# Moving the first tile's routing ahead of the second tile's last work in a two-block transformer kernel

## The reference, cut to what matters

```python
def peer_ffn(h, w_pq, sub_keys, u_tab, v_tab):          # for each token, 8 heads
    q = (xc @ w_pq).reshape(P_CHUNK, P_HEADS, 2, P_DK // 2)
    s = jnp.einsum('thpd,hpkd->thpk', q, sub_keys)
    s_top, i_top = lax.top_k(s, P_TOPK)                  # 16 of 128, for each half
    cand = s_top[..., 0, :, None] + s_top[..., 1, None, :]
    best, ci = lax.top_k(cand.reshape(P_CHUNK, P_HEADS, P_TOPK * P_TOPK), P_TOPK)
    ...
    expert = e1 * N_KEYS + e2
    gate = jax.nn.softmax(best, axis=-1)
    act = jax.nn.gelu(jnp.einsum('thkd,td->thk', u_tab[expert], xc), approximate=False)
    return jnp.einsum('thk,thkd->td', gate * act, v_tab[expert])
```

## Time and profile before

| | |
|---|---|
| median of 3 runs | 2809.44 us |
| lowest and highest | 2790.35 and 2810.88 us |
| profiled execution, its time | 2812.51 us |
| its span, first to last instruction | 2810.9 us |
| mean granted TensorE clock | 0.919 of full speed |
| busy: PE, DVE, ACT, POOL | 82%, 60%, 28%, 26% |
| bytes through DMA | 689.8 MB, of them 536.9 MB gathers |

### The profile page before, as it was taken

The page is one execution under the profiler, slowest core; times in us unless marked ns, Lnnn a source line. Parts: engine busy times, 40 slices in busy tenths (PEclk is TensorE's granted clock), DMA queues, the critical chain, the costliest instruction groups (busy, mean ns, idle before and its releaser), DMA issues.

```text
span 2810.9 us, 25600 instructions
## 1 busy us (share of the span) xinstructions
PE 2308.1 (82%) x8558; PEld 1306.4 (46%) x8558; DVE 1694.6 (60%) x3543; ACT 780.4 (28%) x2164; POOL 717.9 (26%) x584
## 2 busy tenths in 40 slices
PE   8998999999999999999987777778865665665655
PEld 5756468877444445666663444335422222222222
DVE  1132369986116995566366777585575767667444
ACT  2223220001011003466133663142223222222222
POOL 0000033431000003000024343444544444444442
PEclk9999999999999999999999999999977888778778
DMA  4101124444212221001479999999999999999997
GB/s 164 60 30 61 53 90 150 153 157 169 105 57 99 86 77 60 30 1 61 162 293 416 351 367 387 405 420 421 419 420 421 420 420 420 419 420 419 420 420 312
DMA packets 88689, 689.81 MB, mean 245 GB/s; under 512 B 9944, under 2 KB 11736, under 8 KB 13936
## 3 DMA queue, kind: packets, MB, share of 16 engines
q0 software_dynamic: 73728, 536.90, 46.6%
q1 hardware_dynamic: 13392, 146.71, 13.6%
q10 hardware_dynamic: 1440, 4.57, 0.4%
HBM read 684.99 MB, written 3.15 MB: 245 GB/s over the span
## 4 chain that ended last, share of the span: by engine, by line
PE 34%; DMA 31%; DVE 6%; ACT 3%; issue 2%; POOL 2%; ACTq 0%; DVEq 0%
DMA weights<-in_experts,expert 23%; PE psum L467 19%; PE psum L1325 6%; DMA slot<-in_experts,expert 4%; DMA xn<-in_experts,expert 3%; PE psum L1061 2%; DVE weights L2673 2%; POOL weights L2767 1%; PE psum L1198 1%; PE psum L1188 1%; PE psum L1084 1%; PE psum L1220 1%; PE psum L1069 1%; DVE slot L2673 1%; ACT spare_row L1893 1%
## 5 line engine op out<-in xcount | busy, mean ns | idle before, releaser
L1325 PE MATMUL psum<-weights,spare_row 128*64 128x512 f32 x872 | 433.7, 778 | 188.0 <-ACT spare_row L1893 188.0
L1325 PE MATMUL psum<-slot,spare_row 128*64 128x512 f32 x816 | 373.2, 747 | 190.7 <-ACT spare_row L1893 190.4
L2767 POOL DMA_INDIRECT slot<-in_experts,expert x204 | 231.0, 1133 | 485.6 <-PE psum L1325 337.0
L2767 POOL DMA_INDIRECT weights<-in_experts,expert x218 | 236.3, 1084 | 323.0 <-PE psum L1325 287.1
L1883 ACT ACTIVATE hidden<-hidden 128x2 f32<-128x2 f32 (+1 forms) x257 | 52.2, 203 | 893.8 <-DVE hidden L2673 893.6
L1325 PEld LDWEIGHTS psum<-weights,spare_row 128*64 128x64 f32 x872 | 121.6, 162 | 361.5 <-ACT spare_row L1893 298.1
L1325 PE MATMUL psum<-xn,spare_row 128*64 128x512 f32 x360 | 222.2, 751 | 58.1 <-ACT spare_row L1893 58.1
L1325 PEld LDWEIGHTS psum<-slot,spare_row 128*64 128x64 f32 x816 | 107.3, 158 | 338.5 <-ACT spare_row L1893 269.0
L467 PE MATMUL psum<-xnT,weights 128*128 128x264 f32 (+1 forms) x1040 | 247.2, 393 | 3.1 <-DVE up_both L2145 1.5
L467 PE MATMUL psum<-hT,weights 128*128 128x512 f32 x560 | 243.0, 596 | 1.9 <-ACT hT L1371 1.9
L467 PEld LDWEIGHTS psum<-xnT,weights 128*128 128x128 f32 x1040 | 200.5, 195 | 40.2 <-issue 5.0
(11 more groups left out here) (427 smaller groups left out, 3604.3 us busy)
## 6 DMA issues: line engine op xcount, KB each, us to landing
weights<-in_w_mod SPq DMA_DIRECT2D x12, 2048.0 KB, 8.6
weights<-in_w_up SPq DMA_DIRECT2D x11, 2048.0 KB, 8.2
weights<-in_w_in SPq DMA_DIRECT2D x8, 2048.0 KB, 8.2
weights<-in_w_pq SPq DMA_DIRECT2D x8, 2048.0 KB, 10.3
weights<-in_w_out SPq DMA_DIRECT2D x6, 2048.0 KB, 8.6
weights<-in_w_in_t SPq DMA_DIRECT2D x4, 2048.0 KB, 8.1
weights<-in_w_down SPq DMA_DIRECT2D x4, 2048.0 KB, 12.5
weights<-in_w_o_mla SPq DMA_DIRECT2D x4, 2048.0 KB, 10.0
```

Source lines behind the costliest of these rows:

```text
L1325: last = pe.matmul(acc.pair[k.pick_rows(j0 + x), half, :], k.diags[(pick + x) % DIAGS], k.slots[slot][:, D + half * 512:D + (half + 1) * 512],
L2767: pool.indirect_dma_start(k.slots[slot], None, k.A["experts"], bass.IndirectOffsetOnAxis(ap=k.expert[b % 2][:, j:j + 1], axis=0))\
```

## The change

PE, ACT and DVE each do the first tile's queries r = 0, 1, its scores and expert numbers before the last output piece of the second tile (`out2_piece(1, 1)`, `add_out2(1, 1)`), its norm and its transposes. Of the joint queries, four steps (r = 4, 5) instead of eight (r = 4 to 7) stand ahead of the picks; the other 20 go between them, so that `REST_STEPS` is 20 and all of the late chain comes four steps later. The route of batch 2 begins two groups later, since it needs r = 6 to 9. `route` on DVE has one more step, between the expert numbers and the gates.

```diff
--- before.py
+++ after.py
@@ -47,7 +47,7 @@
 BY = P // NARROW
 LATE_PAIR, LATE_LEAD, LATE_PERIOD = 4, 4, 14
 LATE_STEPS = LATE_LEAD + LATE_PERIOD * (AH // 2 - LATE_PAIR - 1) + 20
-REST_STEPS = 16
+REST_STEPS = 20
 DIAGS = 16
 BANK = 512
 LOW = -3.0e38
@@ -237,6 +237,8 @@
 
         if self.finishes(b):
             return 3
+        if b == 1:
+            return 2
         return 4 if b + 1 < len(self.order) and self.order[b + 1][0] == 2 and self.order[b + 1][1] == 0 else 0
 
     def queries_behind(self, c):
@@ -1271,8 +1273,6 @@
         whole(out2_piece(0, 1, wa))
         mod_row(3)
         transposed2(0)
-        whole(out2_piece(1, 1, wb))
-        k.ring_done[unit_a], k.ring_done[unit_b] = ps.of["out2", 0, 1].full[-1], ps.of["out2", 1, 1].full[-1]
         unit, w = weights(KC, 512)
         k.ring.order, k.ring.at = [0, 1], 0
 
@@ -1285,6 +1285,8 @@
         first_queries(0, 0)
         first_queries(0, 1)
         route(0)
+        whole(out2_piece(1, 1, wb))
+        k.ring_done[unit_a], k.ring_done[unit_b] = ps.of["out2", 0, 1].full[-1], ps.of["out2", 1, 1].full[-1]
         first_queries(0, 2)
         first_queries(0, 3)
         transposed2(1)
@@ -1292,7 +1294,7 @@
         for r in range(4):
             first_queries(1, r)
         rest = queries2(0, tiles_, 1)
-        for _ in range(8):
+        for _ in range(4):
             next(rest)
         return rest
 
@@ -1798,7 +1800,6 @@
         norm4(0)
         mod_row(3)
         transposed2(0)
-        norm4(1)
 
         def first_queries(i, r):
             copy_out(("pq", 0, r, i), k.q(r, i), of["pq", 0, r, i].pair[:, 0, 0:P])
@@ -1810,14 +1811,15 @@
         first_queries(0, 2)
         first_queries(0, 3)
         stack(0)
+        norm4(1)
+        for _ in routing:
+            pass
         transposed2(1)
         for r in range(4):
             first_queries(1, r)
-        for _ in routing:
-            pass
         stack(1)
         rest = queries2(0, 4)
-        for _ in range(8):
+        for _ in range(4):
             next(rest)
         return rest
 
@@ -2525,13 +2527,16 @@
         norm4(0)
         add_out2(0, 1)
         transposed2(0)
+        routing = route(0)
+        for _ in range(18):
+            next(routing)
         add_out2(1, 1)
         norm4(1)
+        for _ in routing:
+            pass
+        transposed2(1)
         dve.wait_ge(*of["row", 3].free)
-        for n, _ in enumerate(route(0)):
-            if n == 5:
-                transposed2(1)
-        return k.gap(2 * (2 * PH - 4 - 4))
+        return k.gap(2 * (2 * PH - 4) - 4)
 
     def transposed2(i):
         turn(("h2T", i), k.merged[:, :, i * P:(i + 1) * P], [k.ones[:, 0:1]] * KC)
@@ -2612,6 +2617,7 @@
             for c, dst in enumerate((slice(0, PAIR), slice(PAIR, P))):
                 ins = dve.scalar_tensor_tensor(stacked[0][dst, :, :, a], first[src, :, :, c], float(NKEY), second[src, :, :, c], ALU.mult, ALU.add)
         ins.then_inc(s.expert)
+        yield
         dve.wait_ge(s.gate_exp, b + 1)
         dve.tensor_reduce(k.gsum[:, 0, 0:nh], g, AX_X, ALU.add).then_inc(v.up())
         dve.wait_ge(*v.now())
```

## The result

The changed kernel takes 2816.77 us (median of 20 runs, 2800.13 to 2825.28), the kernel before 2802.82 us in as many runs beside it (2790.35 to 2810.88; two of the three runs shown ahead of the prediction were among its slowest, so their median of 2809.44 stood 6.6 us high). The profiled execution took 2817.1 us, with a span of 2815.8 us at a mean granted clock of 0.916.

A forecast was written before the change was run, and what follows sets the result against it. From slice 20 on, DMA gathers were taken to set the pace. +0.2 (start of the picks) and +2.5 (load), the rest 0, made +2.7 us: 2815.2 against the profiled execution, 2812.1 us against the median; range 2790 to 2826.

The forecast's parts named there:

- rival C: w_pq unit 3's load not absorbed: gathers of groups 4 to 6 late, +7 instead of +2.5, 2816.6 us; chance 0.13.
- First gather: Start of the picks: with the output piece off PE's path, expert numbers and first gather come 7.2 us earlier.
- Tile 1 later: PE: tile 1's queries, behind ACT's stack copies and norm, end 7.0 us later, and so does the fourth gather.
- the clock's term: Slow PE clock after its wait ahead of tile 1's queries: 1.6 us as before, ends -1.6 and +5.9.
- Four steps fewer: Joint queries ahead of the picks halved: 6.99 us saved on PE, paying for tile 1's delay, balance +0.2.
- The load: w_pq unit 3, 2 MiB, moves among gathers: 5.0 us less 2.5 of free DMA, +2.5, ends 0 and 7.
- The late chain: Late attention and the query groups ahead of it, four groups later, at the DMA pace: 0, 3.3 us either way.
- rival S: Rival of the experiments, no chance given: the late chain four groups later, with POOL's slot 10 wait, is the loss.
- rival B: POOL's 8 us wait at slot 10 near 2021 us lets DMA run dry: +8, 2820 us; chance 0.10.
- Rival A: Earlier start carries through, PE's wait for tile 1 not growing: 7.0 us of queries kept, 2802.4 us; chance 0.17.
- Rival D: Late attention's pace changes with what stands beside it: +27 or -27 us; chance 0.10, half to each side.

The follow-up runs named there:

- order alone: Changed kernel's order ahead of the picks, but with all eight query steps before them and the late chain in its old place: ratio 1.0036 against the kernel before.
- steps alone: Kernel before with four query steps ahead of the picks, 20 between them, late chain four groups later, batch 2's route two groups later: ratio 1.0011.
- Fillers: Changed kernel with four more query chains, into a bank nobody reads, in PE's wait ahead of tile 1's transposes: ratio 1.0030 against the kernel before.
- double steps with the stack copies later: Kernel before, four query steps ahead of the picks, two in each of the first four groups, ACT's stack(0) behind its half of transposed2(1): ratio 0.9990.

## Why the prediction was right, and where its terms were not

The time (2816.77) lies in the range, the change is within 1%, and the sign was the forecast's. But the size was +2.7 us where 12 were measured. The forecast of 2812.1 us came within 4.7 us of the time by luck: it starts from the median of three runs, 2809.44, where twenty runs gave 2802.82, and from there +2.7 is 2805.5. Of the rivals, C's mechanism and one that I had priced at zero carried the difference, together with the clock. One reading was off as well: DMA is 90% busy from the 22nd slice on, not from the 20th; nothing in the sum hangs on it.

The two halves of the change, each run alone, say where the sum missed. For the order alone it had +7.0 us; the ratio gives 10 us and the profile 13.2. For the steps alone it had -7.0 and +2.5 for the load, so -4.5; the ratio gives 3 us, with an interval that reaches from -1 to 7, and the profile +1.4. So the saving in steps was real at the first freed slot and gone at the end, and what is left is about the loss of the order.

- **First gather, -7.2:** measured -7.1, at 17.4 us instead of 24.5 behind the anchor. **It is worth nothing by itself**, as far as these runs tell and as forecast: POOL's wait at slot 0 came, 17.91 us.
- **Tile 1 later, +7.0:** +9.1 and +8.1 at the 4th gather. The order on ACT was as I read it. What I had too small is the clock's term. I took 1.6 us as before, with the ends 1.6 lower and 5.9 higher; for the queries it was 2.9 and 1.9 (10.26 and 9.27 against 7.41 warm), which is hardly more than chance, since the kernel before has 1.6 and 2.4 in its two profiles. The 0.9 for the transposes, which I had left warm, came in both profiles. Fillers removed both.
- **Four steps fewer, -7.0:** 7.1 in both directions (steps alone, order alone). The balance at the first freed slot was +3.5 and +1.0 instead of +0.2; 1.4 of the +3.5 is the second fall of the clock, at the first picks, for which the sum has no term.
- **The load, +2.5 with ends 0 and 7:** this is the step whose mechanism was wrong. From the 7th to the 17th gather 4.7 and 5.7 us were lost, 4.1 to 6.7 in all kernels that have the load among the gathers, and 0.6 to 1.0 when it is small. I had set it against DMA's idle 2.5 us, as bytes against bytes. But a load does not choose that gap: it slowed the gathers in front of it, and the 4.7 us that DVE waited for picks 12 and 13 went straight into its route, on whose numbers POOL was waiting already. That is the mechanism of rival C. That C's 2816.6 us is nearly the measured time is luck: C adds 7 us at this place to a base that stood 6.6 us high. No run shows how much of the load's loss at the 17th gather is left at the end. The rule of the Trainium skill, DMA: Bandwidth & Descriptors, "Queues, rings and completion order", that DMA engines take packets from their queues in turn, fits these waits; I had let it favour the upper end only.
- **The late chain, 0 with 3.3 either way:** about +3.5, just past the bound, so a part of rival S holds. The loss did not come where I had looked for it, at the routes, but at the dip near 452 us.
- **POOL's wait at slot 10 (rival B):** it came as computed, 9.94 us against 8, released by the last queries:

```profile
2035.95 0.94 POOL L2773 DMA_INDIRECT weights<-in_experts,expert  x1 [9.94 <-PE psum L1222]
```

and DMA stayed nearly full through it, and the lag in bytes did not grow, so it cost nothing:

```profile
2030.00:2036.00 6.00, 6.00 (x27) 3.64 (x28) 4.11 (x14) 1.54 (x6) 0.05 (x1) 1.00 1.03 426
2036.00:2042.00 6.00, 3.72 (x16) 1.22 (x12) 4.92 (x21) 1.43 (x6) 4.79 (x4) 1.00 0.99 395
```

- **Rival A** (the 7 us kept) did not come, even where the 7th gather was 7.1 us early: steps alone ended at +1.4. Its price of 2802.4 us also left out the load's +2.5, for which its condition gives no reason.
- **Rival D:** the late attention kept its pace: from the 49th to the 101st gather 155.2 us before and 155.8 in the changed kernel, 153.4 and 158.0 in the second profiles, against the 27 us either way of this rival.

No version was shown to beat the kernel before; double steps with the stack copies later, at 0.9990 (0.9973 to 1.0007), comes nearest.

## What to carry to other kernels

In a stage that ends bound by DMA, an earlier first transfer counts only if the next ones follow: add up bytes by a given time, not the time of the first. Before moving a step, list the loads that it releases and ask what each will lie beside; a load hidden in a gap can cost its full time once it slows transfers that a chain is waiting for; here it did up to the 17th gather. And give each engine's idle stretch its second price, the slow clock behind it, for every matmul until the clock is back.

## What the runs showed of the hardware

- A wait of 7.9 us on PE left the clock at 1.2 GHz for some 9 us of work with one short wait (1412.7 to 1422 us); after one of 3.9 us, in the kernel before, it was back 3.6 us into the work, and 5.1 us in the second profile; in the three profiles where PE's waits ahead of tile 1's queries were 1.23 us and less, it stayed at the full level through them.
- The same wait of 2.85 us ahead of the first picks was followed by the lower clock in three of nine profiles (3.53, 3.48 and 2.76 us for eight records) and not in the other six (2.12 us).
- Two executions of the kernel before differed by 10.2 us ahead of the anchor and by 0.5 us over the late gathers, two of the changed kernel by 0.7 and 0.9. Over all fourteen profiles, in which what lies ahead of the anchor is alike, it moved by 14 us. Counting from a common instruction brought out differences of 1 to 2 us, where twenty whole times of each kernel left an interval of 3 us to either side.
- A gather of 1 MiB that 2.5 us of DMA time would move was read 8 us after its issue when only one other was in front of it (double steps with the stack copies later).
